# Expert rounds of a mixture-of-experts layer: one loop body for each pair of experts, sixteen pairs in a row

## The reference, cut to what matters

```
y = (silu(x @ w1[e]) * (x @ w3[e])) @ w2[e]     # x: the tokens of expert e; w1, w3: 1024 x 512, w2: 512 x 1024
```

## Time and profile before

| | |
|---|---|
| median of 3 executions | 3608.04 us |
| the profiled execution's own time | 3597.47 us |
| its span, first to last instruction | 3595.7 us |
| TensorE busy | 3212.1 us (89%), mean granted clock 0.942 |
| VectorE, ScalarE, GpSimd busy | 1459.9, 831.4, 255.5 us |
| expert rounds of layer 0 | 1250.98 to 1932.39 us, 681.4 us |
| expert rounds of layer 1 | 2907.33 to 3537.62 us, 630.3 us |

### The profile page before, as it was taken

The page is one execution under the profiler, slowest core; times in us unless marked ns, Lnnn a source line. Parts: engine busy times, 40 slices in busy tenths (PEclk is TensorE's granted clock), DMA queues, the critical chain, the costliest instruction groups (busy, mean ns, idle before and its releaser), DMA issues. The chain is left out here.

```text
span 3595.7 us, 48176 instructions
## 1 busy us (share of the span) xinstructions
PE 3212.1 (89%) x17267; PEld 1746.3 (49%) x17268; DVE 1459.9 (41%) x4224; ACT 831.4 (23%) x1602; POOL 255.5 (7%) x321
## 2 busy tenths in 40 slices
PE   6999956899999499999997899899999779999983
PEld 3666724744455344444343455477775434444431
DVE  2333255755464411111112688666656421111114
ACT  1111122465511000000001344355551100000000
POOL 0000003400050000000000000000002000000001
PEclk8999978999999699999998999999999889999996
DMA  9700087300042469999783321100003158899998
GB/s 345 266 24 23 18 306 252 88 1 1 1 154 79 183 262 405 358 364 402 283 313 146 106 88 65 71 1 1 1 1 139 50 222 327 316 361 380 404 411 310
DMA packets 283211, 676.92 MB, mean 188 GB/s; under 512 B 24004, under 2 KB 36468, under 8 KB 282996
## 3 DMA queue, kind: packets, MB, share of 16 engines
q1 hardware_dynamic: 252596, 560.12, 41.3%
q0 software_dynamic: 20176, 76.55, 5.8%
q10 hardware_dynamic: 10224, 37.23, 2.5%
HBM read 579.32 MB, written 94.50 MB: 187 GB/s over the span
## 5 line engine op out<-in xcount | busy, mean ns | idle before, releaser
L2583 PE MATMUL ex_ps_g<-w_ring,ex_xT 128*64 128x512 f32 x1696 | 400.3, 627 | 50.4 <-issue 50.4
L2614 PE MATMUL ps_y<-w_ring,ex_hT 128*64 128x512 f32 x1696 | 399.1, 602 | 0.0
L2595 PE MATMUL ps_u<-w_ring,ex_xT 128*64 128x256 f32 x3392 | 387.4, 381 | 0.0
L2595 PEld LDWEIGHTS ps_u<-w_ring,ex_xT 128*64 128x64 f32 x3392 | 243.4, 137 | 142.2 <-issue 38.8
L2583 PEld LDWEIGHTS ex_ps_g<-w_ring,ex_xT 128*64 128x64 f32 x1696 | 128.6, 144 | 292.7 <-issue 292.1
L1670 PE MATMUL of_ps_r<-of_w,cat 128*128 128x512 f32 (+1 forms) x608 | 258.1, 581 | 3.0 <-ACT cat L1753 3.0
L408 PE MATMUL ps_r<-w,hT 128*128 128x512 f32 (+1 forms) x640 | 249.0, 546 | 2.9 <-issue 2.9
L2679 DVE SCALAR_TENSOR_TENSOR ex_hr<-ex_th,ex_ps_g 128x512 f32<-128x512 f32 x53 | 36.5, 688 | 441.2 <-ACT ex_th L2657 441.2
L2614 PEld LDWEIGHTS ps_y<-w_ring,ex_hT 128*64 128x64 f32 x1696 | 107.7, 136 | 177.9 <-issue 177.9
L1397 PE MATMUL mo_ps_o<-mo_w,mo_cT 128*128 128x512 f32 x416 | 185.5, 598 | 1.6 <-DMA mo_w<-in_e_w_out 1.2
L2124 DVE TENSOR_SCALAR_CACHE_REDUCE oa_sx<-oa_ps_s 128x512 f32<-128x512 f32 (+1 forms) x288 | 160.1, 598 | 54.2 <-PE oa_ps_s L2040 53.2
(11 more groups left out here) (495 smaller groups left out, 4326.1 us busy)
## 6 DMA issues: line engine op xcount, KB each, us to landing
w_ring<-in_w SPq DMA_DIRECT2D x768, 512.0 KB, 10.6
ml_staging<-in_w_ada SPq DMA_DIRECT2D x14, 2048.0 KB, 12.4
y_dram<-zeros POOLq DMA_DIRECT2D x2, 14080.0 KB, 65.7
y_dram<-ex_y ACTq DMA_DIRECT2D x53, 512.0 KB, 6.3
ml_spare<-in_w_ada SPq DMA_DIRECT2D x6, 2048.0 KB, 12.6
ml_arena<-ml_rows SPq DMA_DIRECT2D x40, 256.0 KB, 4.2
f_dram<-mo_f SPq DMA_DIRECT2D x18, 512.0 KB, 2.8
w<-in_e_w_in SPq DMA_DIRECT2D x2, 4096.0 KB, 26.0
```

What stands on the lines that cost most here:

```text
L2583: mm = pe.matmul(ps_g[rows, :], xT[:, k, rows], weight(k // 2)[:, h, (k % 2) * DE:(k % 2 + 1) * DE], start=k == 0, stop=k == KD - 1)
L2595: mm = pe.matmul(ps_u[rows, f, 0:256], xT[:, k, rows], weight(4 + k // 2)[:, h, at:at + 256], start=k == 0, stop=k == KD - 1)
L2614: mm = pe.matmul(ps_y[rows, half, :], hT[:, k, rows], weight(8 + k)[:, h, half * 512:(half + 1) * 512], start=k == 0, stop=k == 3)
```

## The change

TensorE's outer loop goes, and the 16 pairs are written one behind the other. Each pair has one copy of the round, in a loop over all its rounds; there is no branch over it and no special last round. So a layer's code holds 16 copies, each passed once or repeated in place. `w_used` is now counted up 12 times in every round, with the mark for chunk 11 on the first matmul of the following round instead of on the 1 by 1 matmul, which goes. SyncE's part is written out for the pairs too; since `w_used` counts rounds, it reads from the table in which round the pair that holds the slot is through, and waits for that round times 12 plus the chunk.

```diff
     @block.sync
     def _(sp):
-        def pair(i, u):
-            e = experts_of(sp, R, i * TURN + u)
+        def last_round(pair):
+
+            entry = sp.value_load(R.table[0:1, pair:pair + 1], min_val=0, max_val=32 * 64 - 1)
+            last = entry // 32 + entry % 32 + pair
...
+        for pair in range(1, NPAIR):
+            e = experts_of(sp, R, pair)
             for c in range(PER_PAIR):
...
-                sp.wait_ge(w_used, i * (TURN * PER_PAIR) + (q + 1 - RING))
-                load_chunk(sp, A, layer, R, e, u, c)
-
-        for u in range(TURN):
-            pair(0, u)
-        with sp.Fori(1, NPAIR // TURN) as i:
-            for u in range(TURN):
-                pair(i, u)
+                of, chunk = (q - RING) // PER_PAIR, (q - RING) % PER_PAIR
+                if c == 0 or chunk == 0:
+                    last = last_round(of)
+                sp.wait_ge(w_used, last * PER_PAIR + (chunk + 2))
+                load_chunk(sp, A, layer, R, e, pair, c)
...
-        def round_of(i, u, gb, last):
+        def round_of(pair, gb):
             def take(c):
 
-                q = u * PER_PAIR + c
-                pe.wait_ge(R.w_in[q % RING], i * (USES * 32) + (q // RING + 1) * 32)
+                q = pair * PER_PAIR + c
+                pe.wait_ge(R.w_in[q % RING], (q // RING + 1) * 32)
...
             def used(mm):
 
-                if last:
-                    mm.then_inc(w_used, 1)
+                mm.then_inc(w_used, 1)
...
-                    if k % 2 == 0 and h == 0 and k:
+                    if k % 2 == 0 and h == 0:
                         used(mm)
...
-            if last:
-
-                pe.matmul(ps_t[0:1, 0:1], g.ident[:, 0:1], g.ident[:, 0:1], start=True, stop=True).then_inc(w_used, 1)
...
-        with pe.Fori(0, NPAIR // TURN) as i:
-            for u in range(TURN):
-                entry = pe.value_load(R.table[0:1, bass.ds(i * TURN + u, 1)], min_val=0, max_val=32 * 64 - 1)
...
-                with pe.If(more > 0):
-                    with pe.Fori(0, more) as b:
-                        round_of(i, u, nc.s_assert_within(start + b, 0, MAXB - 1, skip_runtime_bounds_check_because="MAXB rounds at most"), False)
-                round_of(i, u, nc.s_assert_within(start + more, 0, MAXB - 1, skip_runtime_bounds_check_because="MAXB rounds at most"), True)
+        for pair in range(NPAIR):
+            entry = pe.value_load(R.table[0:1, pair:pair + 1], min_val=0, max_val=32 * 64 - 1)
...
+            with pe.Fori(0, rounds) as b:
+                round_of(pair, nc.s_assert_within(start + b, 0, MAXB - 1, skip_runtime_bounds_check_because="MAXB rounds at most"))
```

More of the change, by code:

```diff
@@ L2473, in experts @@
     tag = f"ex{layer}_"
-    TURN = RING // math.gcd(RING, PER_PAIR)
-    USES = TURN * PER_PAIR // RING
     def s(name):
@@ L2502, in _ @@
     def _(sp):
-        def pair(i, u):
-            e = experts_of(sp, R, i * TURN + u)
+        def last_round(pair):
+            entry = sp.value_load(R.table[0:1, pair:pair + 1], min_val=0, max_val=32 * 64 - 1)
+            last = entry // 32 + entry % 32 + pair
+            return nc.s_assert_within(last, 0, MAXB - 1, skip_runtime_bounds_check_because="MAXB rounds at most")
+        for pair in range(1, NPAIR):
+            e = experts_of(sp, R, pair)
             for c in range(PER_PAIR):
-                q = u * PER_PAIR + c
-                if isinstance(i, int) and i == 0 and q < RING:
+                q = pair * PER_PAIR + c
+                if q < RING:
                     continue
-                sp.wait_ge(w_used, i * (TURN * PER_PAIR) + (q + 1 - RING))
-                load_chunk(sp, A, layer, R, e, u, c)
-        for u in range(TURN):
-            pair(0, u)
-        with sp.Fori(1, NPAIR // TURN) as i:
-            for u in range(TURN):
-                pair(i, u)
+                of, chunk = (q - RING) // PER_PAIR, (q - RING) % PER_PAIR
[3 more added lines that the diff above has]
+                load_chunk(sp, A, layer, R, e, pair, c)
     @block.gpsimd
@@ L2559, in turn_h @@
             mm.then_inc(h_turned, 1)
-        def round_of(i, u, gb, last):
+        def round_of(pair, gb):
             def take(c):
-                q = u * PER_PAIR + c
-                pe.wait_ge(R.w_in[q % RING], i * (USES * 32) + (q // RING + 1) * 32)
+                q = pair * PER_PAIR + c
+                pe.wait_ge(R.w_in[q % RING], (q // RING + 1) * 32)
             def weight(c):
-                return R.w[:, (u * PER_PAIR + c) % RING, :, :]
+                return R.w[:, (pair * PER_PAIR + c) % RING, :, :]
             def used(mm):
-                if last:
-                    mm.then_inc(w_used, 1)
+                mm.then_inc(w_used, 1)
             pe.wait_ge(x_act, gb + 1)
@@ L2630, in _ @@
         pe.wait_ge(R.tabled, 1)
-        with pe.Fori(0, NPAIR // TURN) as i:
-            for u in range(TURN):
-                entry = pe.value_load(R.table[0:1, bass.ds(i * TURN + u, 1)], min_val=0, max_val=32 * 64 - 1)
-                before = nc.s_assert_within(entry // 32, 0, MAXB - NPAIR, skip_runtime_bounds_check_because="MAXB rounds at most, one each for the pairs")
-                more = entry % 32
-                start = before + (i * TURN + u)
-                with pe.If(more > 0):
-                    with pe.Fori(0, more) as b:
-                        round_of(i, u, nc.s_assert_within(start + b, 0, MAXB - 1, skip_runtime_bounds_check_because="MAXB rounds at most"), False)
-                round_of(i, u, nc.s_assert_within(start + more, 0, MAXB - 1, skip_runtime_bounds_check_because="MAXB rounds at most"), True)
+        for pair in range(NPAIR):
+            entry = pe.value_load(R.table[0:1, pair:pair + 1], min_val=0, max_val=32 * 64 - 1)
+            start = nc.s_assert_within(entry // 32, 0, MAXB - NPAIR, skip_runtime_bounds_check_because="MAXB rounds at most, one each for the pairs") + pair
+            rounds = nc.s_assert_within(entry % 32 + 1, 1, 32, skip_runtime_bounds_check_because="each pair has a round")
+            with pe.Fori(0, rounds) as b:
+                round_of(pair, nc.s_assert_within(start + b, 0, MAXB - 1, skip_runtime_bounds_check_because="MAXB rounds at most"))
     @block.scalar
```

## The result

The changed kernel took 3549.74 us (median of 4 executions, 3542.16 to 3555.16) against 3609.82 us for the kernel before on the same chip: a ratio of 0.9839, 95% interval 0.9818 to 0.9860. The forecast was 3554.5. A second measurement, on another occasion, gave 3553.1 against 3604.2, ratio 0.9850 (0.9837 to 0.9863). The profiled execution has a span of 3544.7 us, 51.0 less than before; so the profile shows 51 of the 51 to 60 us that the medians show.

The account below looks back on a forecast made before the run. TensorE plus its interruptions, mostly far sequencer jumps, was taken to bound the expert stages; 31.7 us (layer 0) + 22.5 (layer 1), less about 0.7, made 53.5, so 3608.0 - 53.5 = 3554.5 us, range 3542 to 3571.

Parts of the forecast that it names:

- Layer 0, 31.7 us: Layer 0's expert rounds: long branches, their gaps, slow products behind and small matmuls go, the slow first round stays; 31.7 us.
- Layer 1, pairs 0 to 10, 21.6 us: Layer 1's first 11 pairs: 485.7 us for 20 rounds needing 463.0, less 1.1 for the slow start; 21.6 us gained.
- the tail, 0.9: Layer 1, pairs 11 to 15: weight stream bounds next, so layer 1 gives 22.5 in all; rival, not stream-bound, chance 0.05.
- the 2.3: End of layer 1: last weights forecast to land at 3512.3 us, the last round to end at 3514.6.
- 23.0 us in the working: Layer 1's whole gain as worked out, 3537.6 - 3514.6 = 23.0 us, before 22.5 was taken.
- The stream elsewhere, zero: Pairs alternating one and two rounds: weights need 68.7 us against TensorE's 69.5, so no loss; stream rival, chance 0.08.
- Jumps back over one round, zero: Every pair's loop branch, 21 jumps in all, costs zero; rival that they miss at 5.5 us each, chance 0.05.
- Code in sequence: The 16 copies in a row need about 20 instruction packets, none late; rival that gaps return, chance 0.05.
- SyncE and the marks, at most 2 us: SyncE's extra table loads and register instructions, and chunk 11's later mark: zero, at most 2 us; about 0.7 set aside.
- Two signs that did not come as written: Layer 0's rounds ending near 1901 us of the span; layer 1's last round ending 54 us earlier than before.

Follow-up runs that it names:

- eight copies: Changed kernel with TensorE's outer loop put back as 2 turns of 8 pairs, 8 single copies a turn, no skip; ratio to before 0.9899 (0.9872 to 0.9925).
- small matmul in every round: Changed kernel with a 1 by 1 matmul at the end of every round, 53 in all, marking nothing; ratio to before 0.9885 (0.9870 to 0.9900).
- small pair first: Changed kernel with pairs exchanged two by two, the pair with fewest rounds first, then the one with most; 3539.6 us, ratio to before 0.9820.
- SyncE written out alone: Kernel before with only SyncE's loop over the pairs written out, w_used counted as before; ratio to before 1.0003 (0.9992 to 1.0014).
- outer loop written out: Kernel before with only TensorE's outer loop written out, both round copies, skip and 1 by 1 matmul kept; ratio to before 0.9923 (0.9906 to 0.9941).

## Why the prediction was right

**Layer 0, 31.7 us.** Measured 681.4 - 649.9 = 31.5. The parts are in the traces: idle time behind far jumps and long skips, 19.1 us; slow products behind three of the five gaps (9.49, 9.71 and 9.90 us for 7.09), 7.8; the sixteen small matmuls at 0.27, 4.3; together 31.2. The eight copies show the first two as the work of a far jump, and the small matmul in every round shows the third.

**Layer 1, pairs 0 to 10, 21.6 us, and the tail, 0.9.** Measured 630.3 - 609.2 = 21.1 in sum. Pair 11 begins at:

```profile
3342.53 7.04 PE L2583 MATMUL ex_ps_g<-w_ring,ex_xT 128*64 128x512 f32 x32
```

So pairs 0 to 10 took 464.5 us against 485.7, 21.2 less, and the tail gave nothing: 3487.3 - 3342.5 = 144.8 us against 144.6. What sized the sum was the last weight DMA. After, with the granted clock behind TensorE's last wait below it:

```profile
L2468 SPq DMA_DIRECT2D w_ring<-in_w x13: 379/1007/2234, 3453.8 to 3467.8; - x13
...
DMA to landing us min/median/max: 9.9/11.4/14.2
```
```profile
3472.05:3476.17 4.12, 4.12 (x25) 2.31 (x26) 0.42 (x1) 0.00 (x0) 0.00 (x0) 0.67 1.03 420
```

The last issue comes 3467.8 - 2878.1 = 589.7 us into the stage against 3519.4 - 2907.3 = 612.1 before, 22.4 us earlier, where 21.6 was forecast. The last landing, 3467.8 + 14.2 = 3482.0, is 603.9 us into the stage against 626.6 before, 22.7 earlier. It is 5.3 us before the end, and I had said 2.3. Two sizes were off. The last four chunks landed in 3482.0 - 3472.0 = 10.0 us, not 4 x 2.8 = 11.2, so the last wait ended later, counted from the last landing, by the same 1.2. And the 24 up products behind that wait took 4.12 us at a granted clock of 0.67, where they took 2.81 behind the single wait in the row of the small pair first: after a series of waits TensorE was slower, which the sum had at full speed. These two are 2.5 of the 3.0 us by which the 2.3 was short, and the earlier landing gives back 1.1: 23.0 us in the working became 23.0 - 3.0 + 1.1 = 21.1.

**The stream elsewhere, zero.** Right: no wait for the ring in layer 0 nor in pairs 0 to 12 of layer 1; in the first profile they begin at 3397.65, in pair 13. The margin of 0.8 us for two pairs was enough.

**Jumps back over one round, zero.** Right: 0.231 us at most in 21 jumps. The Trainium skill's rule ("Runtime: NRT & Kernel Launch", section "Instruction fetch mechanics") is right in that a far jump waits for code, as the 5.98 us and the packet within them show; of how far, the runs show more room on TensorE than two pages of 256 instructions: some 1180 instructions are kept.

**Code in sequence.** 19 and 18 packets, for about 20 expected, and no late one.

**SyncE and the marks, at most 2 us.** Not seen apart; SyncE written out alone gave 1.0003.

**The total.** 53.5 us were forecast; the spans say 51.0, the two comparisons of medians 60.1 and 51.1. The 9 us between the two comparisons are less than the spread of the kernel before alone (3598.5 to 3618.5 us over the comparisons), so the profile's 51 is the better number for the mechanism, and the 2.5 us it is short of the forecast are 0.2 in layer 0, 1.4 in layer 1 and 1.6 in the rest of the program, less the 0.7 set aside for marks and register work. That the forecast of 3554.5 us came so close to 3549.7 and 3553.1 is partly the luck of this spread.

**Two signs that did not come as written.** Layer 0 ended at 1906.5 us of the span and not near 1901, because its stage began 5.7 us later than before (1256.63 for 1250.98); why it did is not shown. And the last round ended 3537.6 - 3487.3 = 50.3 us earlier, not 54.

**What is not settled:** which place makes a skip of 295 instructions long. The kernel before had 7 long of 15 taken and the one with the outer loop written out 4 of 15. The rule by block borders explained only part of it.

## What to carry to other kernels

When idle time on an engine has no releaser, look at the sequencer's own branches: by its length in instructions alone a loop may be free or cost the sequencer 6 us a turn, of which TensorE stood idle for some 4 here, and a branch over code may cost the same. Keep one copy of a long body in a short loop rather than write its last turn out apart for the sake of a semaphore count. Every turn can count, and the engine that waits can compute the number that it needs; SyncE does so here. And before counting a removed stall as gain, ask what lands just before the work behind it: here 29 of the 50 us that TensorE lost in layer 1 only passed the time until the weights came, and a better order of the pairs then gave 9.5 us more where no branch was left to mend.

## What was not expected of the hardware

TensorE's gate products were not slow behind every gap: after gaps of 3.2 to 4.4 us they took 7.09 us in some places (3246.90 with eight copies, at 3.94 us of idle time) and 8.5 to 10.1 in others, so a stall cost its own length at one place and 1.8 times that at another (3.52 + 2.80 us at 3511.33). And a jump back over 1180 instructions of TensorE is as cheap as over some 290 (0.233 and 0.231 us at most).
